# Entry to the experts of a two-block transformer kernel: other loading order and places for weights, gate row folded into the output matrix, gather spread over four banks

## The reference

```
y = sigmoid(ga) * (attn @ w_ao) + sigmoid(gf) * (four @ w_fo)
x = x + g1 * (y @ w_o)                       # g1: one row of 1024 gains
h = rmsnorm(x, norm2_g) * (1 + sc2) + sh2
# 2 of 16 experts per token, weights from a softmax of the router
moe = sum_e gate[e] * (silu(h @ w1[e]) * (h @ w3[e])) @ w2[e]
x = x + g2 * moe
return rmsnorm(x, final_g)
```

## Time and profile before

| | us |
|---|---|
| median of 3 runs | 1150.88 |
| lowest, highest | 1150.53, 1152.21 |
| span of the profiled execution | 1149.7 |
| PE busy in it | 1106.4 |
| DVE, ACT, POOL busy in it | 594.9, 447.8, 25.1 |
| moved in it | 254.88 MB |

### The profile page before, as it was taken

The page is one execution under the profiler, slowest core; times in us unless marked ns, Lnnn a source line. Parts: engine busy times, 40 slices in busy tenths (PEclk is TensorE's granted clock), DMA queues, the critical chain, the costliest instruction groups (busy, mean ns, idle before and its releaser), DMA issues.

```text
span 1149.7 us, 20459 instructions
## 1 busy us (share of the span) xinstructions
PE 1106.4 (96%) x8828; PEld 905.1 (79%) x8828; DVE 594.9 (52%) x803; ACT 447.8 (39%) x570; POOL 25.1 (2%) x30
## 2 busy tenths in 40 slices
PE   6999999899998999999999999999999999999995
PEld 6999998899877758999999999988889653434342
DVE  5545546689644186654555474267557541322122
ACT  6333334764431126433335332367583520211112
POOL 0000000000212010000000000000000000000000
PEclk9999999999999999999999999999999999999999
DMA  9665565454475853665655243333336799999994
GB/s 342 208 189 190 192 193 185 138 174 147 168 295 184 297 191 120 190 193 189 194 184 184 73 148 111 111 111 110 111 114 256 292 405 406 394 424 420 422 420 194
DMA packets 119992, 254.88 MB, mean 222 GB/s; under 512 B 6113, under 2 KB 91377, under 8 KB 107378
## 3 DMA queue, kind: packets, MB, share of 16 engines
q1 hardware_dynamic: 118722, 249.14, 60.7%
q10 hardware_dynamic: 1200, 4.71, 1.2%
HBM read 252.78 MB, written 1.06 MB: 221 GB/s over the span
## 4 chain that ended last, share of the span: by engine, by line
PE 86%; DMA 5%; DVE 5%; ACT 3%; issue 1%; SPq 0%; ACTq 0%; DVEq 0%
PE ps L705 55%; PE ps L684 29%; DMA arena<-in_w_exp_up 4%; ACT arena L1411 2%; DMA ring<-in_ffn_gate 1%; DVE ring_r L2051 1%; PE ps L1163 1%; DVE arena L2103 1%; ACT L1411 0%; PE ps L693 0%; DVE arena L2118 0%; PE ps L1364 0%; PE ps L877 0%; ACT arena_r L1411 0%; DVE arena L2592 0%
## 5 line engine op out<-in xcount | busy, mean ns | idle before, releaser
L705 PE MATMUL ps<-hall_r,arena_r 128*128 128x256 f32 x1760 | 325.5, 283 | 4.5 <-DVE hall_r L1956 4.5
L1950 DVE TENSOR_TENSOR ring_r<-ring,arena_r 128x2048 fp32r<-128x2048 f32 x89 | 203.7, 2291 | 181.3 <-ACT arena_r L1411 179.2
L705 PE MATMUL ps<-arena_r 128*128 128x256 f32 (+1 forms) x1216 | 283.9, 323 | 1.2 <-DVE arena_r L2342 1.2
L705 PEld LDWEIGHTS ps<-hall_r,arena_r 128*128 128x128 f32 x1760 | 275.1, 189 | 6.4 <-issue 3.0
L1411 ACT ACTIVATE arena_r<-ring 128x2048 fp32r<-128x2048 f32 x100 | 190.9, 1914 | 164.6 <-PE ps L705 155.1
L705 PE MATMUL ps<-hall_r,ring_r 128*128 128x256 f32 x880 | 246.9, 281 | 0.0
L705 PEld LDWEIGHTS ps<-arena_r 128*128 128x128 f32 x1216 | 202.6, 188 | 19.7 <-DVE arena_r L2342 1.4
L1411 ACT ACTIVATE arena<-ps 128x512 f32<-128x512 f32 (+3 forms) x133 | 77.9, 599 | 330.9 <-PE ps L705 188.6
L684 PE MATMUL ps<-arena 64*64 64x32 f32 (+7 forms) x2232 | 192.3, 304 | 8.4 <-DMA arena<-in_w_exp_up 2.9
L684 PEld LDWEIGHTS ps<-arena 128*64 128x64 f32 (+3 forms) x2232 | 119.2, 143 | 68.1 <-issue 59.5
L705 PEld LDWEIGHTS ps<-hall_r,ring_r 128*128 128x128 f32 x880 | 168.4, 191 | 0.9
(11 more groups left out here) (251 smaller groups left out, 1008.8 us busy)
## 6 DMA issues: line engine op xcount, KB each, us to landing
ring<-in_w_in SPq DMA_DIRECT2D x35, 1024.0 KB, 5.2
arena<-in_w_exp_down SPq DMA_DIRECT2D x32, 1024.0 KB, 13.0
ring<-in_w_mod SPq DMA_DIRECT2D x24, 1024.0 KB, 5.6
ring<-in_ffn_gate SPq DMA_DIRECT2D x22, 1024.0 KB, 5.3
ring<-in_ffn_up SPq DMA_DIRECT2D x22, 1024.0 KB, 5.4
ring<-in_ffn_down SPq DMA_DIRECT2D x22, 1024.0 KB, 5.0
arena<-in_w_exp_up SPq DMA_DIRECT2D x16, 1024.0 KB, 14.3
ring<-in_w_exp_gate SPq DMA_DIRECT2D x16, 1024.0 KB, 9.8
```

The costliest lines, as they stand in the source:

```text
L705: m = pe.matmul(out_, w[i], h[j], start=start and i + j == 0, stop=stop and j == 1, skip_group_check=group)
L1950: tt(lo(n), slot(n), hi(n), ALU.subtract).then_inc(S("w_lo"), 1)
```

## The change

Five things change. (1) SP's order before the first turn: pieces 11 and 6 go to their places right after the attention, piece 1 of the second set no longer waits for x, and pieces 5 and 4 of the second set are new. (2) `TWICE` is 6, so there are 18 places; the two new ones consist of two halves each (a block of the arena and a piece of the constants, a block of the arena and `gb[:, 0, :]`) and are loaded with two DMAs of 512 KB each. (3) g1 is no longer applied by DVE: POOL multiplies each of the four pieces of w_out_2 by the row in its ring slot, and ACT's `split` of these waits for that (`o2_gained`). DVE then adds the product to x in one step. (4) The gather writes banks 2, 3, 0, 1 and signals after every second k; it waits for `rounds` in its middle, since bank 0 holds the counts. (5) The final gain is made after the last turn by two matmuls with a row of ones and two ACT copies. Small tiles (router scratch, low part of y, high parts) move to other blocks, and some semaphores are shared.

```
-        PAIR, TWICE = 12, 4
+        PAIR, TWICE = 12, 6
...
+            if u and m == 4:
+                return [A(8), cst[:, CONSTS["dft_d"][0]:CONSTS["dft_d"][0] + D]]
+            if u and m == 5:
+                return [A(10), gb[:, 0, :]]
...
             load_expert(10, 0)
+            load_expert(11, 0)
+            sp.wait_ge(*W("att_o", 8))
+            load_expert(6, 0)
             for c in range(2):
                 load(N_O2 + c, r256("w_out_2", c))
...
                 load_expert(m, 0)
                 if m == 1:
+                    load_expert(0, 0, 1)
                     sp.wait_ge(*W("y_mix", 4))
                     load_expert(8, 0)
-            load_expert(6, 0)
-            load_expert(11, 0)
-            sp.wait_ge(*W("w_used", N_AO + 4))
-            load_expert(0, 0, 1)
-            sp.wait_ge(*W("x4_done", 4))
-            load_expert(1, 0, 1)
+                if m == 2:
+                    sp.wait_ge(*W("o2_gained", 4))
+                    load_expert(5, 0, 1)
+                if m == 3:
+                    load_expert(4, 0, 1)
+                if m == 4:
+                    load_expert(1, 0, 1)
...
-            sp.dma_start(gb[:, 0, :], a["rows"][:, 0:D].broadcast_to([P, D])).then_inc(S("final_gain"), 16)
...
-            pool.wait_ge(*W("heads_sq", 16))
-            pool.memset(c_pad[:, :, :], 0.0).then_inc(S("w_zero"), 1)
+            pool.wait_ge(*W("gates_kept", 16))
+            for c in range(4):
+                n = N_O2 + c
+                pool.wait_ge(*W(f"w_in_slot{n % RING}", 16 * (n // RING + 1)))
+                pool.tensor_tensor(rows(n), rows(n), gb[:, 0, :].unsqueeze(1).broadcast_to([P, 2, D]),
+                                   ALU.mult).then_inc(S("o2_gained"), 1)
+                if c == 0:
+                    pool.wait_ge(*W("heads_sq", 16))
+                    pool.memset(c_pad[:, :, :], 0.0).then_inc(S("w_zero"), 1)
...
-            for b, ks in enumerate(((0, 1, 4, 5), (2, 3, 6, 7))):
-                for j, k in enumerate(ks):
-                    for t in range(TT):
-                        m = mm(ps[:, 2 + b, j * P:(j + 1) * P], xn[:, t, k * P:(k + 1) * P], pick_0[:, t, :],
-                               start=t == 0, stop=t == 1)
-                m.then_inc(S("gathered"), 1)
-            pe.wait_ge(*W("rounds", 1))
+            for k in range(KT):
+                if k == 4:
+                    pe.wait_ge(*W("rounds", 1))
+                for t in range(TT):
+                    m = mm(ps[:, (2, 3, 0, 1)[k // 2], (k % 2) * P:(k % 2 + 1) * P], xn[:, t, k * P:(k + 1) * P],
+                           pick_0[:, t, :], start=t == 0, stop=t == 1)
+                if k % 2:
+                    m.then_inc(S("gathered" if k >= 4 else "first_rows"), 1)
...
+            for h in range(2):
+                mm(ps[:, h, :], ones[0:1, :], row_f[:, h * 512:(h + 1) * 512]).then_inc(S("gain_rows"), 1)
...
-                act.wait_ge(*W(f"w_in_slot{n % RING}", at(16 * (n // RING + 1), it, 16 * per // RING)))
+                if N_O2 <= n < N_EXP:
+                    act.wait_ge(*W("o2_gained", n - N_O2 + 1))
+                else:
+                    act.wait_ge(*W(f"w_in_slot{n % RING}", at(16 * (n // RING + 1), it, 16 * per // RING)))
...
             fetch(ACT.Sqrt)
+            for h in range(2):
+                act.wait_ge(*W("gain_rows", h + 1))
+                f(gb[:, 0, h * 512:(h + 1) * 512], ps[:, h, :], ACT.Copy).then_inc(S("gain_kept"), 1)
...
-                    link(tt(gated[:, t, s], ps[:, 2 * t + h, :], gb[:, 0, s], ALU.mult))
-                    tt(x[:, t, s], x[:, t, s], gated[:, t, s], ALU.add).then_inc(S("x4_done"), 1)
+                    tt(x[:, t, s], ps[:, 2 * t + h, :], x[:, t, s], ALU.add).then_inc(S("x4_done"), 1)
```

More of the change, by code:

```diff
@@ L267, in rows, with exp_rows @@
             return slot(n).rearrange("p (k n) -> p k n", k=2)
-        PAIR, TWICE = 12, 4
+        PAIR, TWICE = 12, 6
         def exp_slot(m, u):
+            if u and m == 4:
+                return [A(8), cst[:, CONSTS["dft_d"][0]:CONSTS["dft_d"][0] + D]]
+            if u and m == 5:
+                return [A(10), gb[:, 0, :]]
             if u and m < TWICE:
-                return (hall[:, 0].rearrange("p k n -> p (k n)"), A(6, SLOT),
-                        hall[:, 1].rearrange("p k n -> p (k n)"), x[:, :, :].rearrange("p t n -> p (t n)"))[m]
+                return [(hall[:, 0].rearrange("p k n -> p (k n)"), A(6, SLOT),
+                         hall[:, 1].rearrange("p k n -> p (k n)"), x[:, :, :].rearrange("p t n -> p (t n)"))[m]]
             if m < RING:
-                return slot(N_EXP + m)
-            return A(11 + 2 * (m - RING), SLOT)
+                return [slot(N_EXP + m)]
+            return [A(11 + 2 * (m - RING), SLOT)]
+        def exp_rows(m, u):
+            n = 512 if m < 8 else 1024
+            return [part[:, j:j + n] for part in exp_slot(m, u) for j in range(0, part.shape[-1], n)]
         def exp_loaded(m, u):
@@ L558, in load_expert @@
                 src = w.rearrange("(q i) c p k n -> q i c p k n", i=4)[bass.ds(four, 1), 2 * u + m % 2, c, :, :, :].squeeze(0)
-                sp.dma_start(exp_slot(m, u).rearrange("p (k n) -> p k n", k=src.shape[1]), src).then_inc(
-                    exp_loaded(m, u)[0], 16)
+                parts = exp_slot(m, u)
+                n = src.shape[1] // len(parts)
+                for j, part in enumerate(parts):
+                    sp.dma_start(part.rearrange("p (k n) -> p k n", k=n), src[:, j * n:(j + 1) * n, :]).then_inc(
+                        exp_loaded(m, u)[0], 16)
             def next_ones(pair, u, four):
@@ L1312, in expert_weight @@
                 sem, before = exp_loaded(m, u)
-                pe.wait_ge(sem, pair * 16 + (before + 16) if m < TWICE else nth(before + 16, pair, u, 16))
+                each = 16 * len(exp_slot(m, u))
+                pe.wait_ge(sem, pair * each + (before + each) if m < TWICE else nth(before + 16, pair, u, 16))
             def gather_two(ks):
@@ L1340, in turn @@
                         if w == 0:
-                            pe.wait_ge(*W("h_sel_v", pair * 4 + (8 if u else 2 * c + 2)))
+                            pe.wait_ge(*W("h_sel_v", pair * 4 + (8 if u else 4)))
                             pe.wait_ge(*W("h_sel_a", pair * 4 + (8 if u else 2 * c + 2)))
-                        two = [exp_slot(4 * w + 2 * c + e, u).rearrange("p (k n) -> p k n", k=4) for e in range(2)]
+                        two = [exp_rows(4 * w + 2 * c + e, u) for e in range(2)]
                         for e in range(2):
@@ L1384, in turn @@
                 for c in range(2):
-                    two = [exp_slot(8 + 2 * c + e, u).rearrange("p (k n) -> p k n", k=2) for e in range(2)]
+                    two = [exp_rows(8 + 2 * c + e, u) for e in range(2)]
                     for e in range(2):
@@ L1392, in turn @@
                                        hs_t[:, 2 * c + f, e * SLOTS:(e + 1) * SLOTS],
-                                       two[e][:, f, h * 512:(h + 1) * 512], start=c == 0 and f == 0,
+                                       two[e][f][:, h * 512:(h + 1) * 512], start=c == 0 and f == 0,
                                        stop=c == 1 and f == 1, group=True)
@@ L1882, in select @@
                       ACT.Identity, scale=mod(3, k), bias=mod(2, k)).then_inc(S("h_sel_a"), 1)
-            act.wait_ge(*W("gathered", 3))
-            for j, k in enumerate((2, 3, 6, 7)):
-                f(h_sel[:, k, 1, :], ps[:, 3, j * P:(j + 1) * P], ACT.Identity, scale=mod(3, k),
-                  bias=mod(2, k)).then_inc(S("h_sel_a"), 1)
+            for k in (2, 3, 6, 7):
+                act.wait_ge(*(W("gathered", 3) if k >= 4 else W("first_rows", 2)))
+                f(h_sel[:, k, 1, :], ps[:, 1 if k >= 4 else 3, (k % 2) * P:(k % 2 + 1) * P], ACT.Identity,
+                  scale=mod(3, k), bias=mod(2, k)).then_inc(S("h_sel_a"), 1)
             f(xn_hi, xn, ACT.Copy).then_inc(S("xn_hi"), 1)
@@ L2527, in _ @@
             v.tensor_copy(n_rounds.bitcast(U32), rt(22, 1)).then_inc(S("rounds"), 1)
-            v.wait_ge(*W("gathered", 2))
-            for j, k in enumerate((0, 1, 4, 5)):
-                ts(h_sel[:, k, 1, :], ps[:, 2, j * P:(j + 1) * P], mod(3, k), mod(2, k), ALU.mult,
-                   ALU.add).then_inc(S("h_sel_v"), 1)
+            for k in (0, 1, 4, 5):
+                v.wait_ge(*(W("gathered", 2) if k >= 4 else W("first_rows", 1)))
+                ts(h_sel[:, k, 1, :], ps[:, 0 if k >= 4 else 2, (k % 2) * P:(k % 2 + 1) * P], mod(3, k), mod(2, k),
+                   ALU.mult, ALU.add).then_inc(S("h_sel_v"), 1)
             for r in range(1, 4):
```

33 lines of the change are left out of this document (23 added, 10 removed).

## The result

The changed kernel takes **1157.45 us** (median of 13 runs, 1155.1 to 1160.84), the one before 1152.07 in the same measurement (13 runs, 1150.53 to 1156.42). The ratio is 1.0046, with a 95% interval of 1.0033 to 1.0059: slower by 5.4 us. Forecast was +2.45 us on the 1150.88 of three runs, 1153.3, with a range that ended at 1156.0. The profiled execution of the changed kernel has a span of 1153.9 us, that of before 1149.7.

A forecast was written before the change was run, and what follows sets the result against it. PE's dense products, the chain from 908 to 924.5, four weight waits of 4.9 us and ACT's chain at the end bound the kernel; -1.4 + 4.0 - 1.15 + 1.0 = +2.45 gave 1153.3 us, range 1149.0 to 1156.0.

The forecast's parts named there:

- Part 1: DVE's chain before the first turn: two adds instead of four instructions for the gate row, -1.4 us.
- Part 3: The gather before the first turn: ACT and DVE copy halves earlier, so PE goes on sooner, -1.15 us.
- Part 2: POOL's four multiplications by the gate row: DVE takes turns with POOL on SBUF, PE is late, +4.0 us.
- rival B: POOL's multiplications: no contention with DVE for these shapes, so they are hidden, 1149.3 us; chance 0.25.
- Each turn: DVE's subtraction waits for a POOL multiplication; PE late by 0.6 at the third chunk and 0.8 at the fourth.
- the first late start: PE at w_attn_out's second chunk: DVE's subtraction waits for POOL's first multiplication, PE stands 0.3 to 0.7 us.
- The last turn: PE at w_out's first piece: DVE's add and two low parts stand behind POOL's fourth multiplication, PE late by 2.1 us.
- Part 4: Earlier loads and the two added places: PE's four waits for weights, 4.9 us, stay; effect 0.
- Rival C: Weight loads: the added places remove PE's waits, 4.9 less than A or B, 1148.4 or 1144.4 us; chance 0.10.
- Part 5: The end: two copies from PSUM go between ACT's table load and its squares, +1.0 us.
- D: POOL's multiplications: slower, say 5 us per instruction, 7.4 us in all, 1156.7 us; chance 0.07.

The follow-up runs named there:

- x9: x4 with the gather of the kernel before: two banks, one wait each for DVE and ACT, wait for `rounds` behind it; 1150.99 us, ratio 0.9985.
- x1: Changed kernel without the multiplication by the gate row, on POOL or anywhere; POOL only waits and counts; 1150.71 us, ratio 0.9984.
- x2: Changed kernel with three POOL memsets to an unused block in place of each multiplication, gate row left out; 1151.04 us, ratio 0.9990.
- x10: x4 with PE made to wait for a POOL memset ahead of the first product with w_out; 1155.35 us, ratio 1.0036.
- x4: Changed kernel with the four multiplications by the gate row done by DVE in its gaps, not by POOL; 1150.17 us, ratio 0.9992.
- x8: x5 with the final gain loaded by a DMA after the last turn, not by two matmuls and ACT copies; 1145.2 us, ratio 0.9934.
- x7: x4 without the two added places (16) and with SP's two refill lines exchanged for pair 1; 1149.0 us, ratio 0.9982.
- x5: x4 with SP's two refill lines exchanged for pair 1, so the second set is refilled before the first; 1146.25 us, ratio 0.9954.

## Why the prediction was wrong, by its steps

**Part 1 and Part 3** (-1.4 and -1.15): the stretch from the first matmul that turns x to the first turn went from 16.34 us to 13.93, -2.41 for a predicted -2.55. Part 1's share is 1.43, since x9, which has Part 1 alone, has a chain of 71.48 for 72.91. Part 3's is 0.98. Both are right; Part 3 let PE go on 3.85 us after the gather's start and it was 4.05, since PE stood 0.21 between the gather and the first turn.

**Part 2** (+4.0) is **the step that failed**, in its size. The mechanism is the predicted one, with its places and its order: DVE and POOL took turns, PE was late four times, the last time the most. The rival B, no contention, is out by x1 and x2. The row that it was decided by the earlier trace rows was a tensor_scalar, with one tile and a column of `vec` as inputs, not a tensor_tensor with two tiles; that both stand alike is what the runs added. The term is 5.85 us for 4.0. Three things in it were too small, all in the same direction:

- One POOL instruction. I took 4.1 us, from the row of 512 columns and a fixed part worked out from two memsets. It measured 4.64 for the first and 4.34 and 4.35 for the next two (PE's restarts less 2.29). Each turn then is 4.34 + 2.29 - 5.65 = 0.98 instead of the 0.6 to 0.8 predicted; 0.97 and 0.99 were measured. A fixed part taken from memsets was no evidence for a tensor_tensor; four times the row of 1090 ns, which I had called the upper bound, was nearly the value. The Trainium skill has a figure for this shape ("GPSIMD Engine Reference", section "Elementwise — side-by-side cycle accounting"), 4497 ns for an add of 2048 columns, which lies between the measured ones; I hadn't weighed it, and by it, as an estimate, a turn would cost PE 1.1.
- The first one's start. I let the first piece land 4.9 to 5.5 us after its issue, since the queue was nearly idle. Counted from the first product with w_four_out, POOL began 0.64 us later than the 862.8 that I used. With 0.54 more for its length, and 0.24 since PE asked at 868.66 and not at 868.9, the first late start was 1.63 instead of 0.3 to 0.7.
- The last turn, predicted 2.1, was 2.26.

**The clock.** The profiled execution lost 1.65 us to a low granted clock at 890, which no part of the prediction had. Whether the late starts brought it is open (x10). Over the executions nothing shows it: the thirteen of the changed kernel have a mean clock of 0.9925, and those of x1 and x4, without POOL's work, 0.9924 and 0.9923. Single executions of one kernel differ by the clock: x4's twelve took 1148.35 us at a mean clock of 0.996 and 1154.83 at 0.988. At a mean clock of 0.995 a straight line through the executions gives spans of 1154.0 for after and 1150.0 for the 78 of before that stand beside the experiments (1149.8 to 1150.4 by group), +4.0; the parts measured above (5.85 - 2.41 + 0.31 + 0.98) make +4.7. These 78 have a mean clock of 0.9941. By the slope of the line, 0.7 us for each 0.001, the difference to 0.9925 is 1.1 us, so that +4.0 becomes +5.1 as an estimate, near the median's +5.4. The clocks of the thirteen runs of before behind that median aren't on record, and beside x8 and x9 the kernel before had 0.9928 too, so this is a likely reason and not a shown one.

**Part 4** (0): right. The waits for weights are 2.8 + 1.2 + 1.0 = 5.0 us for 4.9, the stretch with the hole shows a share of 0.54 for 0.87; x4 to x7 show the reason. Rival C, which had them removed, is out, though with two lines exchanged it comes true (x5).

**Part 5** (+1.0): right, 0.98 from the last turn's last matmul to the end of the span; the two copies stand where they were expected, 1.06 us, and x8 takes them away.

**The sum and the range.** With the measured parts the sum is -2.41 + 5.85 + 0.31 + 0.98 = +4.7, and the span of 1149.7 would have become 1154.4; the executions at equal clock have 1154.0. Of the 4.15 us between forecast and result, 1.85 are Part 2, 0.4 the other parts, and 1.2 that the kernel before took 1152.07 us in thirteen runs for the 1150.88 of the three that I started from; the rest, 0.7, is no more than the clock does from one execution to another. Without the 1.85 the result would have been inside the range, without the 1.2 alone it would not. The range ended at 1156.0 because I gave D only 0.07. D was "POOL is slower, 5 us each", with 7.4 us for Part 2, and the truth (4.3 to 4.6 each, 5.85) lies between it and the forecast; that the median lies above D's 1156.7 is the other terms and the base, not D. A price that stands four times in series on the path, and that came from scaling one row by four, deserved a wider range upward.

## What to carry to other kernels

Work that is moved to POOL is hidden only if it reads nothing from SBUF while DVE has instructions with two SBUF operands on the path; otherwise each such DVE instruction can stand for one of POOL's, and PE pays for what the two take together beyond its own work on a chunk (4.34 + 2.29 - 5.65 here). So cut POOL's into short ones (quarters took 6.7 us down to about 1.3) or let DVE do it in its gaps (0 here). More places for weights gain nothing where the order of the refills leaves the queue dry before a fixed event: look for the hole in the DMA share, and change the order and the places together (x7 closed the hole with too few places, and 3.5 us of waits stayed). A price for an operation that is missing from the trace should be scaled from the same operation on the same engine, with no fixed part borrowed from another.

## What the runs showed of the hardware

An instruction that stands behind the lock on SBUF shows as busy: DVE's rows read 19.16 us for three instructions of 2.29. A profile that counts busy time alone would show DVE as the limit there; the POOL rows beside it tell the truth.

In these traces the granted clock falls to half beside idle times of PE, but not beside each, and so at one place in one execution and at another in the next. It was at half from 350 to 354 in before, 890 to 894 in after, 344 to 351 and 371 to 375 in x10, and in x5 from 348 to 362 and 375 to 379; ten of the twelve profiles have it between 344 and 365, for 3.4 to 17 us. The two at 371 and 375 stand behind idle times of 0.6 and 0.5 us, which the other profiles have as well. Here is the changed kernel at one of them, after PE had stood for 2.00 us at 887.3 to 889.3, and x4 at 350, where PE had stood for 2.72 us up to 348.97:

```profile
891.00:892.00 1.00, 1.00 (x3) 0.78 (x3) 1.00 (x1) 1.00 (x2) 0.00 (x0) 0.50 0.96 401
```
```profile
350.00:353.00 3.00, 3.00 (x47) 1.75 (x47) 0.00 (x0) 0.60 (x1) 0.00 (x0) 0.60 0.02 5
```

Three microseconds of it cost 1.4 to 1.7 us, as much as a whole part of this change is worth. A comparison of two single profiles has to take them out before it says anything about 2 us. Why one idle time brings it and another of the same length doesn't, these runs leave open.
